# Reordering the calls of four engines around the attention heads of a two-layer kernel

## The reference

```python
h = rms_norm(x, pre_w); proj = h @ w_in
o_sb = stick_breaking(q_sb, k_sb, v_sb) * silu(sb_gate)            # 8 heads of 64
q, k, v = silu(causal_depthwise_conv(gdn_qkv))                     # 4 heads of 128
m   = strict(beta * (k @ k.T) * decay)                             # per chunk of 64
sol = triangular_solve(I + m, [v * beta, k * beta * exp(g)])       # u, w
intra = lower(q @ k.T * decay)
# per chunk: v_new = u - w @ S; o = q exp(g) @ S + intra @ v_new; S = S exp(g_last) + ...
o_g = rms_norm(o, gdn_norm_w) * silu(gdn_gate)
merged = sigmoid(merge_sb) * (o_sb @ w_sb) + sigmoid(merge_gdn) * (o_g @ w_gdn)
x = x + rms_norm(merged @ w_out, post_w)
```

```python
h = rmsnorm(x, ln_attn_pre); proj = h @ w_in
ad = softmax(s1 + bias) - lam * softmax(s2 + bias)                 # "diff": 4 heads of 2 x 64
sf = q @ k.T / 8 + cum_q - cum_k; of = softmax(sf) @ v             # "fox": 8 heads of 64
x = x + rmsnorm(concat(rmsnorm(ad @ v), of) @ w_out, ln_attn_post)
u = relu(rmsnorm(x, ln_mlp_pre) @ w_up) ** 2                       # width 4096
x = x + rmsnorm(u @ w_down, ln_mlp_post)
```

## Time and profile before

| what | value |
|---|---|
| median of three runs | 1261.82 us (1259.36 to 1261.91) |
| profiled execution, own time | 1260.71 us |
| its span in the profile | 1259.4 us, 15193 instructions |
| busy, share of the span | TensorE 94%, its weight loads 75%, VectorE 46%, ScalarE 45%, GpSimd 37% |
| mean granted clock of TensorE | 0.963 of full speed |
| DMA, mean over the span | 76 GB/s; 95.17 MB |
| chain that ended last | TensorE 79%, VectorE 11%, ScalarE 4%, issue 2%, GpSimd 2%, DMA 1% |

### The profile page before, as it was taken

One profiled execution on the slowest core, in us unless ns is written; L12 is line 12 of the kernel. 1 busy time (PEld: TensorE's weight loads), 2 busy tenths in 40 slices (PEclk: granted clock), 3 DMA queues, 4 the chain that ended last, 5 costly groups with the idle time before them and its releaser, 6 DMA issues.

```text
span 1259.4 us, 15193 instructions
## 1 busy us (share of the span) xinstructions
PE 1184.5 (94%) x5847; PEld 939.3 (75%) x5847; DVE 574.9 (46%) x1124; ACT 571.6 (45%) x1044; POOL 459.8 (37%) x251
## 2 busy tenths in 40 slices
PE   6998898898998999989999999989899999999997
PEld 6776776776776688878676767657788888888886
DVE  4538768778646514244324343341721111644444
ACT  5554665665566663234344444442532222433332
POOL 3253252352351253553222222222544444644441
PEclk9998998998999999999998999987899999999999
DMA  8132121121221233532121211111223332333211
GB/s 232 59 81 54 33 69 34 35 67 34 65 70 34 51 101 100 201 84 67 38 56 46 66 37 67 51 51 51 67 85 100 100 96 91 132 100 101 87 64 67
DMA packets 139802, 95.17 MB, mean 76 GB/s; under 512 B 8801, under 2 KB 124874, under 8 KB 139730
## 3 DMA queue, kind: packets, MB, share of 16 engines
q1 hardware_dynamic: 136112, 88.98, 24.2%
q10 hardware_dynamic: 3618, 5.22, 1.3%
HBM read 91.29 MB, written 2.88 MB: 75 GB/s over the span
## 4 chain that ended last, share of the span: by engine, by line
PE 79%; DVE 11%; ACT 4%; issue 2%; POOL 2%; DMA 1%; SPq 0%; DVEq 0%; ACTq 0%
PE bank L412 23%; PE bank L1160 12%; PE bank L1142 12%; PE bank L441 5%; PE bank L802 4%; PE bank L811 3%; PE bank L827 2%; PE bank L940 2%; PE bank L1173 1%; POOL ring L2393 1%; PE bank L952 1%; DVE s L2009 1%; DVE bank L1927 1%; DVE multipliers L1925 1%; DVE g L1834 1%
## 5 line engine op out<-in xcount | busy, mean ns | idle before, releaser
L2393 POOL TENSOR_TENSOR ring<-raw_ring,ring 128x1024 fp32r<-128x1024 f32 x159 | 390.3, 2459 | 654.7 <-ACT ring L1186 654.7
L412 PE MATMUL bank<-hT,ring 128*128 128x512 f32 x1536 | 417.2, 416 | 4.8 <-POOL ring L2393 2.8
L412 PEld LDWEIGHTS bank<-hT,ring 128*128 128x128 f32 x1536 | 288.1, 196 | 73.3 <-issue 15.2
L1186 ACT CAST ring<-raw_ring 128x1024 fp32r<-128x1024 f32 x160 | 166.7, 1044 | 116.9 <-PE bank L1160 93.8
L1160 PE MATMUL bank<-ring,ring_u 128*128 128x512 f32 x672 | 154.0, 391 | 0.0
L1142 PE MATMUL bank<-hT,ring 128*128 128x512 f32 x672 | 152.5, 389 | 0.0
L1160 PEld LDWEIGHTS bank<-ring,ring_u 128*128 128x128 f32 x672 | 126.2, 188 | 27.6
L1142 PEld LDWEIGHTS bank<-hT,ring 128*128 128x128 f32 x672 | 126.1, 188 | 26.1
L2370 DVE TENSOR_TENSOR ring_u<-u,ring_u 128x1024 fp32r<-128x1024 f32 x32 | 82.4, 2583 | 76.0 <-ACT ring_u L1758 76.0
L2375 DVE TENSOR_TENSOR u<-u 128x512 f32<-128x512 f32 x32 | 22.9, 715 | 139.2 <-ACT u L1765 139.2
L441 PE MATMUL bank<-hT,ring 128*128 128x256 f32 x576 | 70.4, 284 | 2.9 <-DVE hT L1804 2.9
(11 more groups left out here) (295 smaller groups left out, 1632.0 us busy)
## 6 DMA issues: line engine op xcount, KB each, us to landing
raw_ring<-in_w_in SPq DMA_DIRECT2D x144, 256.0 KB, 3.3
raw_ring<-in_w_up SPq DMA_DIRECT2D x64, 256.0 KB, 3.1
raw_ring<-in_w_down SPq DMA_DIRECT2D x64, 256.0 KB, 2.8
raw_ring<-in_w_out SPq DMA_DIRECT2D x32, 256.0 KB, 2.8
x<-in_x SPq DMA_DIRECT2D x4, 512.0 KB, 5.7
raw_ring<-in_w_branch_sb SPq DMA_DIRECT2D x8, 256.0 KB, 2.9
raw_ring<-in_w_branch_gdn SPq DMA_DIRECT2D x8, 256.0 KB, 3.3
x<-in_x ACTq DMA_DIRECT2D x4, 512.0 KB, 5.6
```

Source lines behind the costliest of these rows:

```text
L412: p = pe.matmul(bank, m.slab_k8(n % 4)[:, a, k, :], m.hT[:, b, k, :], start=term == 0, stop=term == 23)
L1186: act.copy(m.ring[:, q, 0, :], m.raw_ring[:, q, :]).then_inc(s.slab_hi[q], 1)
L2393: pool.tensor_tensor(m.ring[:, q, 1, :], m.raw_ring[:, q, :], m.ring[:, q, 0, :].bitcast(F32), ALU.subtract).then_inc(s.slab_lo[q], 1)
```

## The change

The change moves calls and removes or adds none. In TensorE's list, nearly every `tiles.to(n)` around the heads has another number, and some calls change places: in the heads of the first block the gram product comes after term 38 for 48, the first product of level 4 after 84 for 87, that of level 6 after 118 for 111, `delta_solve` after 142 for 132. In VectorE's list for heads 0 to 2, `least` and `delta_rows` stand behind `delta_substitute` for ahead of it, one memset is moved ahead of it, and one `delta_conv` is moved ahead of level 5, one behind level 6. On ScalarE decay copies, exponentials and `tile_a` copies change places. GpSimd's `split` and `delta_masks` change places, and one `split` goes behind level 5. The head beside the merge gates, both groups of heads in the second block, the small products for gates, the order at the start of the kernel and two `split_u` calls ahead of the end of the MLP (ScalarE) are moved likewise. In the last head of the second block the fillers reach from term 1 to term 72, with the last ones behind the last `fox_mix`; in the kernel before all 72 stand ahead of the second row block's first `fox_av`. Left out of the diff below are the end of the merge head on TensorE, all of it on VectorE and ScalarE, the rest of the second block's lists and the preparation of head 0; they are permutations of the same calls.

```diff
@@ -473,10 +473,10 @@
     tiles = Tall(SLABS_A, 8, tile_a_free(0), 4)
     pe.wait_ge(s.small_dve, 1)
     narrow(m.wab_s.rearrange("p two (k n) -> p two k n", k=8), banks[5]).then_inc(s.small_pe, 1)
-    tiles.to(114)
+    tiles.to(102)
     pe.wait_ge(s.small_dve, 10)
     narrow_rows(m.ab_sums, banks[6]).then_inc(s.small_pe, 1)
-    tiles.to(119)
+    tiles.to(104)
...
@@ -654,62 +654,64 @@
         delta_q_sum(i)
         tiles.to(14)
         stick_z(i, 0)
+        tiles.to(24)
         delta_decay(i)
-        stick_v_rows(i)
-        tiles.to(28)
         delta_decay_rows(i)
-        tiles.to(30)
         stick_weights_T(i, 0, 0)
         stick_weights_T(i, 1, 0)
         delta_k_sum(i)
         delta_v_rows(i)
+        stick_v_rows(i)
+        tiles.to(25)
         stick_z(i, 1)
-        tiles.to(32)
+        tiles.to(28)
         stick_av(i, 0)
-        tiles.to(48)
+        tiles.to(38)
         delta_gram(i)
-        tiles.to(53)
+        tiles.to(49)
+        stick_weights_T(i, 1, 1)
         stick_weights_T(i, 0, 1)
-        stick_weights_T(i, 1, 1)
-        tiles.to(66)
+        tiles.to(58)
+        stick_av(i, 1)
+        tiles.to(67)
         stick_z(i, 2)
-        stick_av(i, 1)
-        tiles.to(87)
+        tiles.to(84)
         delta_level_first(i, 4)
-        tiles.to(89)
+        tiles.to(92)
         delta_level_second(i, 4)
-        tiles.to(103)
+        tiles.to(93)
         stick_weights_T(i, 0, 2)
         stick_weights_T(i, 1, 2)
+        tiles.to(95)
         delta_level_first(i, 5)
-        tiles.to(106)
+        tiles.to(103)
         delta_level_second(i, 5)
+        stick_av(i, 2)
         stick_z(i, 3)
-        tiles.to(109)
-        stick_av(i, 2)
-        tiles.to(111)
+        tiles.to(118)
         delta_level_first(i, 6)
-        tiles.to(117)
+        tiles.to(132)
         delta_level_second(i, 6)
-        tiles.to(132)
+        tiles.to(142)
         delta_solve(i)
-        tiles.to(139)
+        tiles.to(146)
+        stick_weights_T(i, 1, 3)
+        tiles.to(150)
         delta_chunk(i, 0)
-        tiles.to(143)
+        tiles.to(151)
+        stick_weights_T(i, 0, 3)
         delta_from_state(i, 1)
-        stick_weights_T(i, 0, 3)
-        stick_weights_T(i, 1, 3)
-        tiles.to(147)
+        tiles.to(153)
         delta_chunk(i, 1)
-        tiles.to(151)
+        tiles.to(156)
         delta_from_state(i, 2)
-        tiles.to(154)
+        tiles.to(158)
         delta_chunk(i, 2)
         stick_av(i, 3)
         delta_from_state(i, 3)
-        tiles.to(159)
+        tiles.to(160)
         delta_chunk(i, 3)
-        tiles.to(171)
+        tiles.to(168)
         delta_o_sum(i)
         tiles.rest()
@@ -721,65 +723,72 @@
     i = 3
     tiles = Tall(SLABS_MERGE, 16, merge_free)
-    tiles.to(1)
+    tiles.to(14)
     delta_q_sum(i)
-    tiles.to(14)
+    tiles.to(15)
+    stick_v_rows(i)
+    tiles.to(17)
     delta_decay(i)
     tiles.to(19)
     delta_decay_rows(i)
-    tiles.to(30)
-    stick_v_rows(i)
-    tiles.to(41)
+    tiles.to(48)
     delta_k_sum(i)
-    tiles.to(52)
+    tiles.to(63)
     delta_v_rows(i)
-    tiles.to(68)
+    tiles.to(75)
     delta_gram(i)
-    tiles.to(113)
+    tiles.to(98)
     stick_z(i, 0)
-    tiles.to(124)
+    tiles.to(119)
     stick_weights_T(i, 0, 0)
+    tiles.to(133)
     stick_weights_T(i, 1, 0)
     tiles.to(138)
     delta_level_first(i, 4)
     stick_z(i, 1)
+    tiles.to(141)
     stick_av(i, 0)
+    tiles.to(144)
     delta_level_second(i, 4)
-    tiles.to(154)
+    tiles.to(156)
     delta_level_first(i, 5)
-    tiles.to(159)
-    delta_level_second(i, 5)
+    tiles.to(157)
     stick_weights_T(i, 0, 1)
     stick_weights_T(i, 1, 1)
-    tiles.to(163)
+    tiles.to(161)
+    delta_level_second(i, 5)
     stick_z(i, 2)
+    tiles.to(164)
     stick_av(i, 1)
-    tiles.to(166)
+    tiles.to(169)
     delta_level_first(i, 6)
-    tiles.to(179)
+    tiles.to(173)
...
@@ -961,78 +971,76 @@
     for i in range(3):
         tiles = Tall(SLABS_B + 6 * (i + 1), 6, tile_b_free(6 * (i + 1)))
-        tiles.to(13)
+        tiles.to(9)
         diff_v_rows(i, pairs)
-        tiles.to(18)
+        tiles.to(17)
+        diff_z(i, 1, 0, 0, pairs)
+        tiles.to(19)
+        diff_z(i, 1, 0, 1, pairs)
+        diff_z(i, 0, 0, 0, pairs)
         fox_v_rows(i)
-        tiles.to(22)
-        diff_z(i, 0, 0, 0, pairs)
+        tiles.to(24)
+        fox_decay(i, 1)
         diff_z(i, 0, 0, 1, pairs)
-        diff_z(i, 1, 0, 0, pairs)
-        diff_z(i, 1, 0, 1, pairs)
+        tiles.to(36)
         fox_decay(i, 0)
-        fox_decay(i, 1)
-        tiles.to(23)
+        fox_z(i, 1, 0)
+        tiles.to(47)
         fox_z(i, 0, 0)
-        tiles.to(25)
-        fox_z(i, 1, 0)
-        tiles.to(40)
+        tiles.to(60)
         fox_rows_T(i, 0, 0)
-        tiles.to(43)
+        tiles.to(63)
+        diff_rows_T(i, 0, 0, pairs)
+        tiles.to(66)
         fox_rows_T(i, 1, 0)
-        tiles.to(48)
+        tiles.to(71)
         fox_av(i, 0, 0)
-        tiles.to(50)
         fox_av(i, 1, 0)
-        tiles.to(54)
-        diff_rows_T(i, 0, 0, pairs)
-        tiles.to(55)
+        tiles.to(72)
         diff_rows_T(i, 1, 0, pairs)
-        tiles.to(58)
+        diff_av(i, 0, 0, pairs)
         fox_z(i, 0, 1)
+        tiles.to(76)
+        diff_z(i, 0, 1, 0, pairs)
         fox_z(i, 1, 1)
-        diff_av(i, 0, 0, pairs)
         diff_av(i, 1, 0, pairs)
-        tiles.to(68)
+        tiles.to(84)
         fox_rows_T(i, 0, 1)
-        tiles.to(70)
...
@@ -1062,65 +1070,74 @@
     i = 3
     tiles = HeadsOut()
-    tiles.to(15)
+    tiles.to(1)
+    fox_v_rows(i)
     diff_v_rows(i, last_pairs)
-    fox_v_rows(i)
-    tiles.to(22)
+    tiles.to(2)
+    fox_decay(i, 0)
     diff_z(i, 0, 0, 0, last_pairs)
+    fox_decay(i, 1)
+    fox_z(i, 0, 0)
     diff_z(i, 1, 0, 0, last_pairs)
-    fox_decay(i, 0)
-    fox_decay(i, 1)
-    tiles.to(28)
-    fox_z(i, 0, 0)
-    tiles.to(31)
+    diff_z(i, 0, 0, 1, last_pairs)
     fox_z(i, 1, 0)
-    diff_z(i, 0, 0, 1, last_pairs)
+    tiles.to(6)
+    fox_rows_T(i, 0, 0)
+    tiles.to(11)
+    fox_rows_T(i, 1, 0)
+    fox_av(i, 0, 0)
+    tiles.to(19)
+    fox_av(i, 1, 0)
     diff_z(i, 1, 0, 1, last_pairs)
-    tiles.to(32)
-    fox_rows_T(i, 0, 0)
-    tiles.to(36)
-    fox_rows_T(i, 1, 0)
-    tiles.to(45)
-    fox_av(i, 0, 0)
+    fox_z(i, 0, 1)
+    tiles.to(23)
+    fox_z(i, 1, 1)
+    tiles.to(34)
+    diff_rows_T(i, 1, 0, last_pairs)
+    tiles.to(38)
+    fox_rows_T(i, 0, 1)
+    tiles.to(39)
+    fox_rows_T(i, 1, 1)
+    diff_av(i, 1, 0, last_pairs)
+    tiles.to(42)
+    fox_av(i, 0, 1)
+    fox_av(i, 1, 1)
+    diff_rows_T(i, 0, 0, last_pairs)
+    fox_z(i, 0, 2)
+    tiles.to(43)
+    diff_av(i, 0, 0, last_pairs)
+    diff_z(i, 1, 1, 0, last_pairs)
+    fox_z(i, 1, 2)
+    tiles.to(46)
+    diff_z(i, 0, 1, 0, last_pairs)
+    diff_z(i, 1, 1, 1, last_pairs)
+    fox_rows_T(i, 0, 2)
     tiles.to(48)
...
+    tiles.to(52)
     fox_av(i, 1, 2)
     fox_z(i, 0, 3)
     fox_z(i, 1, 3)
+    tiles.to(53)
+    diff_rows_T(i, 0, 1, last_pairs)
+    tiles.to(55)
+    diff_av(i, 0, 1, last_pairs)
     fox_rows_T(i, 0, 3)
+    tiles.to(56)
     fox_rows_T(i, 1, 3)
-    diff_rows_T(i, 0, 1, last_pairs)
     diff_rows_T(i, 1, 1, last_pairs)
-    diff_av(i, 0, 1, last_pairs)
+    tiles.to(59)
     diff_av(i, 1, 1, last_pairs)
+    tiles.to(60)
     fox_av(i, 0, 3)
+    tiles.to(64)
     fox_av(i, 1, 3)
+    tiles.to(65)
     diff_mix(i, 5)
     fox_mix(i)
+    tiles.to(72)
     pe.wait_ge(s.d_mix, 4)
     pe.wait_ge(s.f_mix, 4)
@@ -1221,17 +1238,17 @@
         norm_squares(0, j, m.x1, m.scr, 0)
     first_squares(0)
+    split(SLABS_A)
+    split(SLABS_A + 1)
     first_squares(1)
     act.wait_ge(s.cols_T, 1)
     act.copy(m.colp[:, 0:73], banks[2][:, 0:73]).then_inc(s.cols, 1)
-    split(SLABS_A)
-    split(SLABS_A + 1)
+    first_squares(2)
     act.wait_ge(s.cols, 1)
     act.wait_ge(s.memsets, 4)
     norm_high(0, 0, m.prew_col)
-    first_squares(2)
+    split(SLABS_A + 2)
     first_squares(3)
-    split(SLABS_A + 2)
     split(SLABS_A + 3)
     norm_high(0, 1, m.prew_col)
@@ -1413,28 +1430,28 @@
         g = 8 * (i + 1)
         delta_q_norm(i)
         stick_soft(i, 0)
-        delta_decay(i)
-        stick_v(i)
         tile_a(g)
         stick_exp(i, 0)
+        delta_decay(i)
         delta_decay_rows(i)
         stick_weights(i, 0)
         delta_k_norm(i)
+        stick_v(i)
         stick_soft(i, 1)
+        stick_exp(i, 1)
+        delta_mT(i)
+        log_of_sigmoid(gate, m.rawg, s.g_sig, 4 * i)
         tile_a(g + 1)
-        stick_exp(i, 1)
-        log_of_sigmoid(gate, m.rawg, s.g_sig, 4 * i)
-        delta_mT(i)
         stick_weights(i, 1)
-        exponential(gate, s.g_dve, 2 * i + 1, s.g_sig)
         tile_a(g + 2)
         stick_soft(i, 2)
+        exponential(gate, s.g_dve, 2 * i + 1, s.g_sig)
         delta_level(i, 4)
         stick_exp(i, 2)
-        tile_a(g + 3)
         stick_gate(i)
```

(29 more changed lines are left out.)

344 lines of the change are left out of this document (162 added, 182 removed).

## The result

The changed kernel takes **1185.07 us** (median of 4 runs, 1183.50 to 1187.09) beside 1260.68 us for the kernel before on the same chip (4 runs): the ratio is 0.9401, 95% interval [0.9382, 0.9421]. The profiled execution took 1183.50 us, with a span of 1182.2. So 77.2 us of the span went where 57.5 were forecast, and the time lies 2.9 us under the low end of the range. The kind of change and its places came as forecast, and the size was too small.

What follows compares the result with a forecast made beforehand. TensorE's idle time and its work at 1.2 GHz were taken as the bound. Gains of 30 + 8 + 11 + 12 less 3.5 gave 57.5 us off 1260.7, so 1204 us on the median, range 1188 to 1238.

Steps and rivals of the forecast that it cites:

- the two links of the inverse: First block: TensorE's worst waits, for VectorE's blocks of the inverse and its last level, 19.9 us together.
- Heads 0 to 2: First block: 10 us a head, from 11.8 (6.6 waits, 5.2 half clock) less 0.5 and 1.3; 30 us together.
- (c): First block, wait before the solve: one convolution goes ahead of level 5, solve ten terms later; an overlapping split costs up to 2.4 us.
- (d): First block, what is late next: the copy of u behind the third convolution, 0 to 1 us late at term 150.
- GpSimd under the convolution: First block, ahead of level 5: one convolution lies under a GpSimd split, which costs up to 2.4 us.
- The merge head: Head beside the merge gates: 8.0 us idle and about 1.9 of half clock; gain of 8 us (3 to 9.5).
- The second block: Its heads 0 to 2: an earlier decay copy removes idle time and half clock; gain of 11 us of 13.7.
- The last head: End of the second block: fillers reach until after the last mix; gain of 12 us, between 18 and 5.
- The start: Kernel start: casts of slabs 0 and 1 ahead of the second row block's squares; cost 3.5 us (2 to 8).
- Rival 1: One link remains late, with waits and half clock left in the heads; 1235 us, chance 0.25.
- nor 2: Rival: TensorE only reaches its waits earlier and the same time reappears elsewhere; 1260 us, chance 0.05.
- nor 3: Rival: the start costs its upper bound of 8 us and rival 2 holds elsewhere; 1269 us, chance 0.08.

Runs made afterwards that it cites:

- e1: The kernel before with the new order of heads 0 to 2 of the first block alone, on all four engines; 1217.63 us.
- e5: The changed kernel with three idle memsets on VectorE just ahead of the blocks of the inverse, heads 0 to 2 of the first block; 1186.88 us.
- e12: The changed kernel with the old start order, first-block transposes of X four terms later and first stick-breaking scores at term 16; 1179.89 us, ratio 0.9347.
- e9: The kernel before, calls of the last head in old order, only its 72 TensorE fillers spread evenly between them, two ScalarE casts later; 1259.48 us.
- e11: The changed kernel with old start order, later transposes of X and stick-breaking scores, and transposes of v ahead of the last head's first filler; 1180.43 us.
- e13: As e12, with seven full-width fillers directly behind the wait at the start of the last head; 1181.21 us, ratio 0.9364.
- e14: The changed kernel with the old order of the start, second series; 1181.96 us, ratio 0.9373.
- E7: The changed kernel with twelve idle memsets on VectorE ahead of the blocks of the inverse, heads 0 to 2 of the first block; 1206.96 us.
- E6: The changed kernel with six idle memsets on VectorE ahead of the blocks of the inverse, heads 0 to 2 of the first block; 1193.94 us.

## Why the prediction was right or wrong

**The reading of what bounds it** was right: idle time and half clock of TensorE, in the stretches named, and the two links of the inverse above all.

**Heads 0 to 2.** The hand timeline of head 1 held to 0.9 us: X was forecast at 196.4 and came at 196.0 (185.73 + 10.28), TensorE at 196.7 and came at 196.6; the second product of level 4 at 199.4 and 199.3; the first of level 6 at 213.4 and 212.5; the solve at 220.7 and 219.8. The copy of u, forecast 0 to 1 us late, was 0.44 early. The step that failed is the sum behind it: "11.8 less 0.5 at its start and 1.3 for (c) and (d)". A head gave 13.1: 7.2 of idle time (8.2 to 1.0) and 5.9 of busy time. The 1.8 us taken off were for lateness that had cover: the order of the first block alone gave the full 39.6 us (e1). The 11.8 itself was 1.3 too low. It left out the head's small waits (0.4 at level 5 and 0.4 at the ring; the idle time fell by 7.2 and not 6.6). It priced the half clock rightly, at 5.2 us (half of the 10.2 us in the trace is 5.1), but busy time fell by 5.9: the rest is busy time at full clock, of the kind that e5 shows with 0.64 us for a wait of 0.62. What makes it is not shown. My upper bound of 37 for three heads, 12.3 a head, was even below the ceiling that I had written down myself, 88.7 - 75.2 = 13.5. This term alone is 9.6 of the 19.7 missed.

**GpSimd under the convolution.** It happened at nearly the bound: 4.30 us for 2.33. It cost nothing, since VectorE's level 5 is ready at 200.50, GpSimd's own part of level 6 at 201.00 (199.25 and 1.75 us), and TensorE asks for both at 202.23. The Trainium skill's rule, SBUF — State Buffer, "Who interferes with whom", agrees with this row for the one multiply-add that began inside the split (2.73 us for 0.75). The outcome that I worked out beside it, 7 us of 10 left in a head, did not come: only one of three collided, and what collides has to be late too.

**The merge head** gave 11.6 for 8: its idle time fell by 7.3 (8.0 to 0.7), near what I wrote, and its busy time by 4.3 where I had seen 1.9 of half clock. The trace has 3.4 us of half clock there, 1.7 us of loss, so the other 2.6 are again busy time at full clock, not explained. From what I had seen I had then taken off more. **The second block** gave 9.3 for 11: idle 1.9 in each head went to 0, as forecast, but busy time fell by only 1.9, 1.4 and 0.4 where my ceiling had 3.1, 3.1 and 1.8 for the clock. A small part of the gap in head 1 is an error of reading: the mean clock of a stretch also counts a wait that lies at 1.2 GHz. There 1.2 of the 6.8 us are TensorE's wait, and the work in it is 5.6 us, a loss of 2.8. Even so 1.3 to 1.5 us in each head did not come (by half of the work at 1.2 GHz, 3.4, 2.8 and 1.7); why was not tested.

**The last head.** Step by step I had 18 and took 12, for fear of short products in its first third. It gave 18.5 in the profiled run and 15.4 where a fall of 6.8 us came (e12); that the profiled run had no fall is luck. The fear named a real thing, as e9 and e11 to e13 show, but its price is 3 us and not 6. **Behind the last head** 1.2 us came that I had not counted: the half clock there is 3.4 us for 6.8. This varies too: in e13 and e14 it was 6.8 again.

**The start** was right: 3.1 for 3.5, squares at 10.70 for 10.8, scaling at 21.02 for 20.5. **Rival 1** (links late, 1235) didn't come, nor 2, nor 3. The rule of the Trainium skill on the clock, TensorE: Matmul & The Clock Gate, "Why this matters for your kernels", asks for no idle gaps above a certain length between bursts. E7 (4.16 us, a fall) and e5 (0.62 us, none) agree with it. E6 does not: its gap of 1.79 us is shorter than those that the page speaks of, and the clock fell in all three heads. Nor does e9: the page has a TensorE that is kept busy at full clock, and here it was busy for 20.5 us at 1.2 GHz. The measurements decide.

**Range.** All discounts went one way, and the low end of 1188 was not even the sum of my own best bounds: 37 + 9.5 + 13.5 + 18 - 2 = 76 gives 1186. The result would have lain 0.7 us under that too. With the ceilings of the stretches (idle plus half clock), 40.5 + 9.9 + 13.7 + 19 - 2, the low end would have been 1181 and held the result.

## What to carry to other kernels

Where TensorE is the bound, price a wait at 1.6 to 2 times its length, as measured here for waits of 0.6 to 4.2 us in one place of this kernel, and set the upper end of the gain near idle time plus half-clock loss of the stretch, read from the rows (the first block gave 39.6 of 40.5, the merge head 11.6 where that sum was 9.9); take nothing off it for lateness that has cover. Move the operand earlier and the consumer later together, since each alone gave 22% and 43% of what both gave. When a step-by-step timeline gives a number, forecast that number, and put the doubt into the range.

## What was not expected of the hardware

Here the half clock came in pieces of 3.4, 6.8 and 10.2 us in most places, and which one comes varies for the same instructions: 49.96 to 53.08 us in the last head, 88.5 to 90.6 in an untouched head. It can begin and last with TensorE fully busy: 20.50 of 20.50 us at 0.50. The spread between runs of one kernel, 2 to 6 us, goes with the half clock: the four runs of the changed kernel took 1183.50, 1184.60, 1185.53 and 1187.09 us at a mean granted clock of 0.994, 0.993, 0.993 and 0.991, and e12's five runs go from 1177.00 us at 0.996 to 1181.41 at 0.991. So single edits under 2 us can only be read in the trace, stretch by stretch.
